# Expert rows turned beside the preceding layer, their norm moved into scores and gelu, second table's rows eight places forward

## The reference, cut to what matters

```
h = h + (g_attn * y_attn + g_rnn * y_rnn) @ w_out          # layer w2_out
x = rms_norm(h, ffn_norm)
q = (x @ w_peer_q)                  # layer w_pq: 8 heads, 2 halves of 128
s = q . subkeys                     # 128 scores for each head and half
experts, best = top 16 of the 256 sums of the two top-16 lists
gates = softmax(best)
act   = gelu(sum_d peer_u[experts] * x)     # 16 rows of 2048 per token and head
out   = sum_k gates * act * peer_v[experts] # 16 more rows
h = h + out
gate = sigmoid(rms_norm(h, ple_norm) @ w_ple_gate)         # layer w2_pg
h = h + gate * (p @ w_ple_proj)                            # layer w2_pp makes p @ w_ple_proj
```

## Time and profile before

| what | us |
|---|---|
| median of 3 runs | 3859.56 (3859.32 to 3861.42) |
| the profiled execution, its own time | 3862.77 |
| its span in the profile | 3861.0 |

### The profile page before, as it was taken

How to read it: one execution, slowest core, us unless ns; L and a number is a source line. 1 busy time by engine, 2 the same in 40 slices (tenths; PEclk the granted TensorE clock), 3 DMA queues, 4 the chain that set the end, 5 groups by cost and what they waited for, 6 DMA issues and landing times.

```text
span 3861.0 us, 53072 instructions
## 1 busy us (share of the span) xinstructions
PE 3285.4 (85%) x20976; PEld 2734.2 (71%) x20976; DVE 2473.2 (64%) x3281; ACT 1432.5 (37%) x2059; POOL 850.5 (22%) x623
## 2 busy tenths in 40 slices
PE   8988998999999999999999996766666667666678
PEld 8977888999999999999998996732222223222248
DVE  6567865654455556874546666977777776555566
ACT  6555555553354444564445452220100001100025
POOL 2000011000000100000000021255665565565522
PEclk9998999999999999999999997878878888888899
DMA  6433243556556565455553456899999999999974
GB/s 227 151 99 110 94 158 120 166 183 188 180 183 189 177 207 176 161 181 185 164 179 101 148 185 221 313 355 421 421 422 421 422 421 420 422 421 421 422 288 148
DMA packets 188024, 952.86 MB, mean 247 GB/s; under 512 B 20992, under 2 KB 21120, under 8 KB 121984
## 3 DMA queue, kind: packets, MB, share of 16 engines
q0 software_dynamic: 73728, 536.90, 33.7%
q1 hardware_dynamic: 114048, 412.56, 33.2%
HBM read 947.29 MB, written 2.10 MB: 246 GB/s over the span
## 4 chain that ended last, share of the span: by engine, by line
PE 57%; DMA 19%; DVE 13%; POOL 4%; ACT 4%; issue 3%; DVEq 0%; ACTq 0%; SPq 0%; POOLq 0%
PE ps L529 56%; DMA BIG<-in_peer_v,CS 7%; DMA HLF<-in_peer_v,CS 6%; DMA HF<-in_peer_v,CS 3%; DVE HL L1755 3%; POOL HLF L511 2%; DVE BIG L1759 2%; POOL BIG L511 2%; DVE BIG L2393 1%; DMA BIG<-in_peer_u,CS 1%; DVE BIG L1755 1%; DMA HLF<-in_peer_u,CS 1%; ACT BIG L1117 1%; ACT HL L1123 1%; PE ps L533 1%
## 5 line engine op out<-in xcount | busy, mean ns | idle before, releaser
L529 PE MATMUL ps<-HS,HL 128*128 128x256 f32 x10128 | 1340.8, 288 | 36.8 <-DVE HL L1755 31.3
L529 PEld LDWEIGHTS ps<-HS,HL 128*128 128x128 f32 x10128 | 1288.0, 196 | 48.6 <-DVE HL L1755 36.2
L1755 DVE TENSOR_TENSOR HL<-RAW,HL 128x1024 fp32r<-128x1024 f32 (+1 forms) x772 | 954.1, 1236 | 246.2 <-ACT HL L1123 181.6
L1123 ACT CAST HL<-RAW 128x1024 fp32r<-128x1024 f32 (+1 forms) x772 | 805.3, 1043 | 499.9 <-PE ps L529 431.8
L529 PE MATMUL ps<-BIGR,HL 128*128 128x256 f32 x6720 | 897.5, 286 | 24.0 <-DVE HL L1755 14.4
L529 PEld LDWEIGHTS ps<-BIGR,HL 128*128 128x128 f32 x6720 | 853.9, 194 | 32.3 <-issue 15.5
L529 PE MATMUL ps<-BIG,HF 128*128 128x512 f32 (+1 forms) x744 | 387.7, 671 | 187.5 <-DMA BIG<-in_peer_v,CS 164.1
L529 PE MATMUL ps<-HLF,HF 128*128 128x512 f32 x648 | 341.1, 679 | 162.1 <-DMA HLF<-in_peer_v,CS 148.8
L529 PEld LDWEIGHTS ps<-BIG,HF 128*128 128x128 f32 (+1 forms) x744 | 158.1, 223 | 412.4 <-issue 378.7
L478 POOL COPY NSUM<-TMP 128x256 f32<-128x256 f32 x6 | 3.3, 552 | 1948.7 <-ACT TMP L1119 1948.7
L2393 DVE CUSTOM_DVE_ANT_0 BIG<-BIG 128x2048 f32<-128x2048 f32 x133 | 304.9, 2293 | 164.1 <-DMA BIG<-in_peer_u,CS 155.1
(11 more groups left out here) (196 smaller groups left out, 2239.6 us busy)
## 6 DMA issues: line engine op xcount, KB each, us to landing
RAW<-in_w_up SPq DMA_DIRECT2D x128, 512.0 KB, 3.8
RAW<-in_w_down SPq DMA_DIRECT2D x128, 512.0 KB, 4.2
RAW<-in_w_out SPq DMA_DIRECT2D x64, 512.0 KB, 3.6
RAW<-in_w_qk SPq DMA_DIRECT2D x32, 512.0 KB, 3.3
RAW<-in_w_xbc SPq DMA_DIRECT2D x32, 512.0 KB, 3.4
RAW<-in_w_xr SPq DMA_DIRECT2D x32, 512.0 KB, 3.4
RAW<-in_w_yr SPq DMA_DIRECT2D x32, 512.0 KB, 3.4
RAW<-in_w_gr SPq DMA_DIRECT2D x32, 512.0 KB, 3.8
```

Of the source, the lines that this page charges most:

```text
L529: return e.matmul(o, l, r, start=start, stop=stop, skip_group_check=True)
L1123: s.done(e.copy(o, i), sig)
L1755: v.done(e.tensor_tensor(o, a, b, op), sig)
```

## The change

HK is made by ScalarE in w2_out's `evac` and without RX, into another part of BIG. Its transposes are steps of w2_out's background (three quarters) and w_pq's (the last quarter), one group per unit, and a transpose of RX itself ("ffn") gives RXC, the factor as one number per token. VectorE no longer makes HK. `evac_pq` moves to ScalarE as a plain copy. The scores are multiplied by RXC when ScalarE copies them (two instructions for one), and the dot products when gelu reads them. `experts` needs no `rowed`; its first route yields after every fourth step. `dot` waits for the last copy to HN. The first v row has place 25 (it was 33), places 0 to 23 take slots 0 to 3, places 24 to 33 slots 0 to 4, and all nine are used from place 34. The stop for the gates of group 0 stands at place 24.

```diff
-TURN = counted([..., ("mla", 16), ("rows", 8)])
+TURN = counted([..., ("mla", 16), ("rows", 8), ("ffn", 1)])
-        PQ, SK, HK = chunks(8192, 8), big(10240, 2048), chunks(14336, 16)
+        PQ, SK, HK = chunks(8192, 8), big(10240, 2048), chunks(15104, 16)
+        RXC = SM[:, 420:422]
@@ the list of gathers and its slots
-            while vs and a >= 16 * vs[0][1] + 17 and (256 - len(vs)) * 224 < (a - 31) * 240:
+            while vs and a >= 16 * vs[0][1] + 17 and (256 - len(vs)) * 232 < (a - 23) * 240:
-            b = q % 4 if q < 32 else (q + 2) % 5 if q < 42 else (5, 6, 7, 8, 4, 0, 1, 2, 3)[(q - 42) % 9]
+            b = q % 4 if q < 24 else q % 5 if q < 34 else (5, 6, 7, 8, 4, 0, 1, 2, 3)[(q - 34) % 9]
@@ TensorE
+                for j in range(4):
+                    yield from until(*(("w2_out", 4 * j + 6) if j < 3 else ("w_pq", 1)))
+                    for i in range(2):
+                        pe.wait_ge(s_hk, 4 * j + 4)
+                        turned([HK[:, c, i * 128:i * 128 + 128] for c in range(4 * j, 4 * j + 4)], TURN["rows"] + 2 * j + i)
+                        yield
+                columns(RX, RXN["ffn_norm"], TURN["ffn"])
+                yield
+            g_row = rows()
+            dense(L["w2_out"], cut_by(mix, s_mix, lambda k: k + 1), None, g_row)
@@ ScalarE
+            def evac_out(c):
+                bank_done(L["w2_out"], c)
+                normed_high("ffn_norm", "ffn_norm", c)
+                act(HK[:, c, :], X[:, c, :], ACT.Identity, (s_hk, c + 1), scale=vec("ffn_norm", c))
-                    copy(SC[:, :, 2 * h:2 * h + 2, :], score_bank(k).rearrange("p (i c n) -> p i c n", i=2, c=2),
-                         sig_score(k))
+                    s.wait_ge(s_tfree, TURN["ffn"] + 1)
+                    for i in range(2):
+                        act(SC[:, i, 2 * h:2 * h + 2, :].rearrange("p c n -> p (c n)"), score_bank(k)[:, i * T:i * T + T],
+                            ACT.Identity, sig_score(k) if i else None, scale=RXC[:, i:i + 1])
             def evac_pq(c):
+                s.wait_ge(s_mm, L["w_pq"].done(c))
+                if c >= 8:
+                    s.wait_ge(s_score, SCORE["score"] + c // 2 - 3)
+                copy(PQ[:, c % 8, :], bank(L["w_pq"], c)[:, 0:T], sig_bank(L["w_pq"], c))
-                    act(d, d, ACT.Gelu_apprx_tanh, (s_gact, n + 1))
+                    act(d, d, ACT.Gelu_apprx_tanh, (s_gact, n + 1), scale=RXC[:, n // 8:n // 8 + 1])
@@ VectorE
-                for c in range(16):
-                    stt(HK[:, c, :], X[:, c, :], vec("ffn_norm", c), RX, ALU.mult, ALU.mult, (s_hk, 1) if c == 15 else None)
+                columns(420, TURN["ffn"])
             def dot(q, n, k):
+                v.wait_ge(s_tfree, TURN["rows"] + 8)
-                    gate_at[max(taken["u", n, 15] + 3, 32) if n < 15 else taken["u", 15, 15] + 1] = n
-                while not rowed[0]:
-                    yield
+                    gate_at[max(taken["u", n, 15] + 3, 24) if n < 15 else taken["u", 15, 15] + 1] = n
                                 step(routes)
+                                steps += 1
+                                if steps % 4 == 0 and not routed[0]:
+                                    yield
             def evac_pq(c):
-                if c >= 8:
-                    v.wait_ge(s_score, SCORE["score"] + c // 2 - 3)
-                scaled(PQ[:, c % 8, :], L["w_pq"], c)
```

More of the change, by code:

```diff
@@ L103 @@
                  ("rglru", 16), ("kr", 1), ("mla", 24), ("score", 8)])
-TURN = counted([("mem", 1), ("rx", 1), ("attn", 16), ("ssd", 16), ("cross", 4), ("mla", 16), ("rows", 8)])
+TURN = counted([("mem", 1), ("rx", 1), ("attn", 16), ("ssd", 16), ("cross", 4), ("mla", 16), ("rows", 8), ("ffn", 1)])
 TURN3 = counted([("qk", 8), ("acs", 2), ("bt", 1), ("xst", 4)])
@@ L996, in tensor @@
             dense(L["w2_ao"], cut_by(os_, s_ofree, lambda k: OUTS["mla"] + k + 1), None, g_ml)
-            dense(L["w2_out"], cut_by(mix, s_mix, lambda k: k + 1))
             def rows():
-                for _ in range(4):
-                    yield
[L1002 to L1008, removed]
+                for j in range(4):
[8 more added lines that the diff above has]
+            dense(L["w2_out"], cut_by(mix, s_mix, lambda k: k + 1), None, g_row)
             def scoring():
@@ L1024, in scoring @@
                     yield
-            g_row, g_sc = rows(), scoring()
+            g_sc = scoring()
             def beside():
                 while True:
-                    step(g_row)
                     step(g_row)
@@ L1046, in value @@
                     pe.wait_ge(s_sfree[1], SCORE["score"] // 2 + 4)
-                    pe.wait_ge(s_tfree, TURN["rows"] + 8)
+                    pe.wait_ge(s_tfree, TURN["ffn"] + 1)
                     pe.wait_ge(s_ofree, OUTS["mla"] + 16)
@@ L1634, in scalar @@
             s.wait_ge(s_qp, 8)
-            dense(L["w2_out"], residual("ffn_norm", L["w2_out"]))
-            norm_end("ffn_norm", L["w_pq"])
             def rows():
[L1639 to L1643, removed]
+                for j in range(4):
+                    yield from until(*(("w2_out", 4 * j + 6) if j < 3 else ("w_pq", 1)))
+                    for i in range(2):
+                        t = TURN["rows"] + 2 * j + i + 1
                         s.wait_ge(s_turn, t)
                         copy(HN[:, i, 512 * j:512 * j + 512], tr_bank, (s_tfree, t))
-                        if j % 2:
-                            yield
+                        yield
+                yield
+            def evac_out(c):
+                bank_done(L["w2_out"], c)
+                normed_high("ffn_norm", "ffn_norm", c)
+                act(HK[:, c, :], X[:, c, :], ACT.Identity, (s_hk, c + 1), scale=vec("ffn_norm", c))
+            g_row = rows()
+            dense(L["w2_out"], evac_out, g_row)
+            norm_end("ffn_norm", L["w_pq"])
             def scoring():
@@ L1738, in vector @@
             have, begun, ready, attended, late, xr, scanned, pq = {}, [False], [0], [False, False], [False], [0], [0], [0]
-            rowed, routed, found = [False], [False], [0]
+            routed, found = [False], [0]
             def until(name, n):
@@ L2320, in vector, with rows @@
             dense(L["w2_ao"], evac_ao, g_ml)
-            dense(L["w2_out"], residual("ffn_norm", L["w2_out"]))
-            norm_end("ffn_norm", L["w_pq"])
-            def rows():
-                v.wait_ge(s_mm, L["w2_out"].end())
-                for c in range(16):
-                    stt(HK[:, c, :], X[:, c, :], vec("ffn_norm", c), RX, ALU.mult, ALU.mult, (s_hk, 1) if c == 15 else None)
[L2328 to L2332, removed]
+            def rows():
+                for j in range(4):
+                    yield from until(*(("w2_out", 4 * j + 6) if j < 3 else ("w_pq", 1)))
+                    yield
+                    yield
+                columns(420, TURN["ffn"])
+                yield
+            g_row = rows()
+            dense(L["w2_out"], residual("ffn_norm", L["w2_out"]), g_row)
+            norm_end("ffn_norm", L["w_pq"])
             def top16(vals, v16, i16):
@@ L2428, in experts @@
             def experts():
-                routes, gate_at = chain(), {}
+                routes, gate_at, steps = chain(), {}, 0
                 for n in range(16):
-                    gate_at[max(taken["u", n, 15] + 3, 32) if n < 15 else taken["u", 15, 15] + 1] = n
-                while not rowed[0]:
-                    yield
+                    gate_at[max(taken["u", n, 15] + 3, 24) if n < 15 else taken["u", 15, 15] + 1] = n
                 for q, (table, n, k) in enumerate(gathers):
@@ L2456, in experts @@
                         yield
-            g_row, g_ex = rows(), experts()
+            g_ex = experts()
             def beside():
                 while True:
-                    step(g_row)
                     step(g_row)
```

## The result

The changed kernel takes 3854.4 us (median of 20 runs, 3851.2 to 3857.4) against 3861.7 (20 runs beside it, 3857.3 to 3866.7). The ratio is 0.9984, 95% interval 0.9978 to 0.9990: by that ratio it is faster by 6.2 us, between 3.9 and 8.5 (the two medians alone lie 7.4 us apart, inside that interval). The forecast was 11.0 us faster, 3848.5 us, with a range for 8 in 10 of 3840 to 3860.

The account below looks back on a forecast made before the run. VectorE's list bounds w_pq, then 1 MB gathers at 421 to 422 GB/s bound the second half. Last row -12.2 and p's transfer +1.2 make -11.0 from 3859.6: 3848.5 us, own range 3843.5 to 3853.5, 8 in 10 3840 to 3860.

Parts of the forecast that it names:

- Part 1: HK's six transpose groups in w2_out: 3.9 us added on TensorE, bounds 0 and 8.0; ScalarE's activation covered.
- Part 2: First route in w_pq: begins at 2345.2 instead of 2358.21, 13.0 us earlier.
- Part 3: From the route to D: VectorE's shorter list in w_pq brings D to 2478.6, 29.6 us earlier.
- D: End of VectorE's `low` of w2_pp's second unit, from which p's transfer hangs; 2508.24 before, forecast 2478.6.
- Part 4: Pause after D: nine slots at D + 41.5, eight more rows left (20.2 us); last row 12.2 us earlier.
- Part 5: p's transfer, 6.0 us before, beside gathers of places 24 to 28: 1.2 us more, bounds 0 and 4.1.
- Part 6: Rest, in the gather stretch: ScalarE's scaled gelu and scores copy, nearer v rows; nothing, at most 3 us.
- (b): p lands 5.0 us late behind two gathers, shifting w2_pp, gelu and gates: 3852.4 us, chance 0.14.
- (c): TensorE at its lower clock bounds w_pq, 5.23 us a unit: 3863.6 us, chance 0.12.
- (a): TensorE hides the transposes (-3.9), first v products run at the higher clock (-2.4): 3842 us, chance 0.12.
- (d): VectorE runs fewer than 24 dots in w_pq: 2.5 us for each missing row, no share of its own.

Follow-up runs that it names:

- four-place kernel: Changed kernel with p fetched early and the first v row at place 29, four places forward instead of eight: 3832.4 us, 0.9930 to before, in both runs.

## Why the prediction was right, and where it was wrong

The direction and the range of 8 in 10 held. The size did not: 11.0 was forecast and 6.2 measured (3.9 to 8.5). The 3854.4 us lie above the forecast's own range, which ended at 3853.5, and within the 0.2% that the prediction gave 0.24, not below it (0.68). Some 2 us of the distance in absolute time are the base: 3859.6 from three runs, 3861.7 from the twenty beside the changed kernel. By its steps:

- **Part 1** (HK beside w2_out): 2.6 us for 3.9. Each of the six groups of four transposes delays the products by 0.43 on average, not by 0.66 (their own rows are 0.60 there): it overlaps the matmuls around it. ScalarE's addition was hidden, and TensorE waited for nobody.
- **Part 2** (the route earlier): 15.3 us for 13.0. Of the 2.3, 1.3 is Part 1's; for the other 1.0 I had added the transposes and the copies end to end.
- **Part 3** (D): 29.4 for 29.6. 24 dots, 1.37 and 2.40 us as counted, 113.6 us from the first dot to D for 113.8. The wait for the first row, which I left at 6.5 us, is 9.3 from the end of the route: 2.8 us that took back the 2.3 of Part 2. That D comes out within 0.2 us is therefore partly luck. That wait also scatters: in the two runs of the four-place kernel its last part was 6.21 and 7.68 us. In the trace the weight loads go on beside these first gathers, since w_pq isn't standing; that they are the reason was not tested.
- **Part 4** (the pause and the eight rows): the mechanism is right in each step, five gathers, the stop at place 24 behind gelu, the slots freed by the v products. Less p's part (7.4 us), the nine slots open 41.3 us after D for the 41.5 counted. 478 rows took 2.52 us each.
- **Part 5** is the step that failed: p's transfer was priced at 1.2 us more and took 7.4 more. I argued that "part of the contention is in the 6.0 already". Hardly any was: with no gather under way the same transfer took 5.8, and in the kernel before one gather had been issued 2.9 us ahead of p. Holding the rows back gave 7.6 us back, and the early fetch removed the wait. With 7.4 in place of 1.2 the sum is -4.8 us, against the -4.0 us that the two traces show from the landmark on.
- **Part 6**: nothing, as said. 421 GB/s to the end in both.

Of the rivals, (b) was the right one, and still too small: it had p 5.0 us late, behind two gathers, and the time at 3852.4. It deserved more than its 0.14. Its rule stands in the Trainium skill (DMA: Bandwidth & Descriptors, section on queues, rings and completion order): an engine works through a packet of one ring before it turns to the next. The runs agree in kind: p took 13.4 us with three gathers issued ahead of it, 11.3 with two, 5.8 with none, and 6.3 when it was issued 0.2 us ahead of all five. From 6.3 to 11.3 and 13.4 that is some 2.4 to 2.5 us for each gather ahead, about what 1 MB takes at 421 GB/s (an estimate from three runs; the weight loads ahead of p were not alike in them). How many packets p waited for no run here shows. Rival (c) fell: PEclk was 0.97 in w_pq and VectorE never waited for TensorE there. Before, TensorE stood for 12.6 us and then in gaps of about 5; from 2375 to 2475 its gaps now are mostly 1.4 and at most 2.2. Of rival (a), only the overlap of the transposes was seen, 1.3 us of its 3.9. Rival (d) had no place: the list was as counted.

What I did not weigh is that the two halves of the change work against each other. The price of the eight rows, 20.2 us, stands in Part 4, but what the change would do with the old list was not worked out. Undoing the eight places alone is worth 16 us, which is more than twice what the whole change gains.

## What to carry to other kernels

When a stage that is bound by an engine's list is shortened ahead of one that is bound by bandwidth, count what each moves: the time at which the queue becomes full, and the units that are then left. Look for a small transfer on which a chain hangs, and for the bulk that is issued just ahead of it. Here an early fetch was worth 17 us, and holding back the large gathers, which nobody needed yet, until the small transfer had landed was worth 8.6, though it added a wait. And where the order of rows is chosen for the old stage lengths, try the change without the new order before taking both.

## What the runs showed of the hardware that was not expected

A transfer of 256 KB took 5.8 us with no gather under way, 6.0 and 7.2 with one gather of 1 MB issued 2.9 and 2.6 us ahead of it, and 11.3 and 13.4 with two and three issued in the 3.5 us ahead of it. It took 6.3 when all five were issued behind it. Groups of four fp32 transposes, 0.60 us by their own rows in w2_out, delayed a busy TensorE by 0.43 us each on average. TensorE's granted clock was 0.97 from 2375 to 2475, with units of 3.1 us and gaps of mostly 1.4 between them. Before it was 0.74 from 2369 to 2435, which takes in the wait of 12.55 us, and 0.87 from 2435 to 2500, with work of four units at a time and waits of about 5 us between.
